# A two-layer network and a conditioned block on one core: the order of the first stage, and the form of the last products

## What is computed

```python
def rmsnorm(x, g):
    y = xf * lax.rsqrt(jnp.mean(xf * xf, axis=-1, keepdims=True) + EPS)
    return (y * g.astype(jnp.float32)).astype(x.dtype)

def pool_mixer(h, w, scale):          # windows 2, 4, 8, 16; a quarter of the columns each
    cs = jnp.cumsum(xg, axis=1)
    outs.append((cs - lag) / cnt - xg)
    ...
    return mixed * scale

def hyena_filters(...):
    hid = jnp.sin(fr * (z @ w1.astype(f32) + b1.astype(f32)))
    hid = jnp.sin(fr * (hid @ w2.astype(f32) + b2.astype(f32)))
...
for i in range(DEPTH):
    a = rmsnorm(h, norm_mix[i])
    h = h + mix
    h = h + swiglu(rmsnorm(h, norm_ffn[i]), ffn_w_gate[i], ffn_w_up[i], ffn_w_down[i])
...
return rmsnorm_2(x, final_g)
```

## Time and profile before

| | us |
|---|---|
| median of 3 runs | 1026.26 (1025.77 to 1027.43) |
| the profiled execution | 1026.83 |
| its span | 1025.0 |
| TensorE busy (matmuls) | 985.7, 96% of the span |
| VectorE busy | 825.7, 81% |
| ScalarE busy | 564.7, 55% |
| GpSimd busy | 110.3, 11% |

### The profile page before, as it was taken

The page is one execution under the profiler, slowest core; times in us unless marked ns, Lnnn a source line. Parts: engine busy times, 40 slices in busy tenths (PEclk is TensorE's granted clock), DMA queues, the critical chain, the costliest instruction groups (busy, mean ns, idle before and its releaser), DMA issues.

```text
span 1025.0 us, 19503 instructions
## 1 busy us (share of the span) xinstructions
PE 985.7 (96%) x7946; PEld 953.8 (93%) x7946; DVE 825.7 (81%) x1388; ACT 564.7 (55%) x1062; POOL 110.3 (11%) x130
## 2 busy tenths in 40 slices
PE   6999999999999999999999999999999999999996
PEld 5999999999888889999999998888999999999995
DVE  7988898887898876999979878888998668776543
ACT  5755454345767656555555535665554466665432
POOL 3100000111000004002203210222001100000001
PEclk9999999999999999999999999999999999999998
DMA  7555557665433334798868814333336436655441
GB/s 239 223 193 212 195 216 255 241 247 206 145 107 120 104 103 166 294 325 302 290 216 298 302 64 160 132 113 111 127 145 209 161 123 221 211 187 182 153 160 42
DMA packets 33881, 192.19 MB, mean 187 GB/s; under 512 B 4976, under 2 KB 6272, under 8 KB 15104
## 3 DMA queue, kind: packets, MB, share of 16 engines
q1 hardware_dynamic: 23440, 157.36, 42.9%
q10 hardware_dynamic: 6912, 25.17, 7.3%
q0 software_dynamic: 3440, 8.42, 2.6%
HBM read 187.78 MB, written 3.15 MB: 186 GB/s over the span
## 4 chain that ended last, share of the span: by engine, by line
PE 70%; DVE 19%; ACT 6%; issue 3%; DMA 2%; POOL 0%; DVEq 0%; ACTq 0%; POOLq 0%
PE ps L93 69%; DVE wl L70 6%; ACT wh L67 2%; DVE a L70 1%; PE ps L96 1%; DMA raw<-w 1%; DVE b L70 1%; ACT s L67 1%; DVE natl L70 1%; DVE s L84 1%; DMA fz<-fz 1%; DVE s L77 1%; DVE xt L73 1%; DVE x L73 0%; DVE x L70 0%
## 5 line engine op out<-in xcount | busy, mean ns | idle before, releaser
L70 DVE TENSOR_TENSOR wl<-raw,wh 128x1024 fp32r<-128x1024 f32 x283 | 341.9, 1223 | 24.4 <-ACT wh L67 23.9
L67 ACT ACTIVATE wh<-raw 128x1024 fp32r<-128x1024 f32 x286 | 296.2, 1049 | 28.3 <-DMA raw<-w 11.1
L93 PE MATMUL ps<-xh,wh 128*128 128x256 f32 (+1 forms) x992 | 278.6, 281 | 3.6 <-DVE wl L70 2.5
L93 PE MATMUL ps<-xh,wl 128*128 128x256 f32 (+1 forms) x992 | 277.1, 279 | 0.0
L93 PE MATMUL ps<-xl,wh 128*128 128x256 f32 x992 | 275.9, 278 | 0.0
L93 PE MATMUL ps<-xt,wh 128*128 128x272 f32 (+1 forms) x1120 | 218.3, 290 | 4.7 <-DVE ps L70 1.5
L93 PEld LDWEIGHTS ps<-xh,wh 128*128 128x128 f32 x992 | 186.9, 188 | 4.8 <-issue 2.4
L93 PEld LDWEIGHTS ps<-xl,wh 128*128 128x128 f32 x992 | 187.3, 189 | 0.0
L93 PEld LDWEIGHTS ps<-xh,wl 128*128 128x128 f32 x992 | 186.9, 188 | 0.2
L93 PEld LDWEIGHTS ps<-xt,wh 128*128 128x128 f32 x1120 | 177.3, 188 | 8.0 <-issue 3.7
L93 PE MATMUL ps<-xt,wl 128*128 128x272 f32 (+1 forms) x560 | 159.9, 286 | 0.0
(11 more groups left out here) (351 smaller groups left out, 1603.6 us busy)
## 6 DMA issues: line engine op xcount, KB each, us to landing
raw<-w SPq DMA_DIRECT2D x141, 1024.0 KB, 5.0
ada<-ada ACTq DMA_DIRECT2D x42, 512.0 KB, 4.5
cb<-ada ACTq DMA_DIRECT2D x6, 512.0 KB, 4.6
raw<-w SPq DMA_DIRECT2D x4, 512.0 KB, 6.3
spare<-w SPq DMA_DIRECT2D x2, 1024.0 KB, 8.6
spectra<-ev POOLq DMA_DIRECT2D x8, 256.0 KB, 3.6
skew<-rpb POOLq DMA_DIRECT2D x8, 192.0 KB, 3.6
x<-x POOLq DMA_DIRECT2D x2, 544.0 KB, 9.5
```

What stands on the lines that cost most here:

```text
L67: return Issued(self.e and self.e.activation(out, src, func, **kw))
L70: return Issued(self.e and self.e.tensor_tensor(out, a, b, op))
L93: return Issued(self.e and self.e.matmul(out, stat, mov, start=start, stop=stop))
```

## The change

- `WARM`, the number of squares of ones, is 13 instead of 20.
- In `start_dve` the sum of squares of token tile 1 comes first, then the four scalings `gw` (with their wait for `cst`), then steps 0 to 2 of the filter network, then the inverse root.
- Steps 3 to 6 of the filter network stand in `first_dve` at f = 0, behind the four `up_out`.
- The output is four VectorE products over two tiles each (128x2x256, `r` repeated for both); GpSimd has none, `final` and its semaphore are gone.

```diff
-WARM = 20
+WARM = 13
...
         V.memset(self.ones[:, :], 1.0 / 1024).then_inc(S["st_v"], ("ones",))
-        for k in range(4):
-            self.mlp_dve(V, 0, k)
         V.wait_ge(S["ld_xt1"], ("load",))
         V.wait_ge(S["st_v"], ("pre",))
         V.ttr(self.sqt[1][:, :], self.xtok[1][:, :], self.xtok[1][:, :], 1.0, 0.0, ALU.mult, ALU.add,
               sm[0:96, 65:66]).then_inc(S["st_v"], ("ssq",))
-        for k in range(4, 7):
+        V.wait_ge(S["ld_cst"], ("load",))
+        for g in range(4):
+            V.ts(sm[:, 88 + 2 * g:90 + 2 * g], self.col("norm_mix0", 2 * g, 2), 1.0 / (2 << g), None,
+                 ALU.mult).then_inc(S["st_v"], ("gw", g))
+        for k in range(3):
             self.mlp_dve(V, 0, k)
...
-        V.wait_ge(S["ld_cst"], ("load",))
-        for g in range(4):
-            V.ts(sm[:, 88 + 2 * g:90 + 2 * g], self.col("norm_mix0", 2 * g, 2), 1.0 / (2 << g), None,
-                 ALU.mult).then_inc(S["st_v"], ("gw", g))
...
             if f == 0:
                 for k in first:
                     self.up_out(V, 0, "f0", self.R[1], T1, *k)
+                for k in range(3, 7):
+                    self.mlp_dve(V, 0, k)
...
         self.rsqrt_dve(V, "out", self.R[0], self.ps[7][:, :TR], TR)
-        for d in range(DT):
-            if d not in (2, 6):
-                self.final(V, d, "out_v")
-
-    def final(self, E, d, done):
-        S, x = self.S, self.x_tile(d, M0, TR)
-        E.wait_ge(S["norm_v"], ("r", "out"))
-        E.wait_ge(S["out_a"], ("x", d))
-        E.tt(x, x, self.R[0][:, :TR], ALU.mult).then_inc(S[done], ("y", d))
+        x = self.X[:, :].rearrange("p (d t) -> p d t", d=DT)
+        for d in range(0, DT, 2):
+            y = x[:, d:d + 2, M0:]
+            V.wait_ge(S["norm_v"], ("r", "out"))
+            V.wait_ge(S["out_a"], ("x", d + 1))
+            V.tt(y, y, self.R[0][:, :TR].unsqueeze(1).broadcast_to([128, 2, TR]), ALU.mult).then_inc(
+                S["out_v"], ("y", d))
...
             self.norm_acc(G, "out", d, TR)
-        for d in (2, 6):
-            self.final(G, d, "out_g")
...
-            for i in (d, d + 1):
-                D.wait_ge(S["out_g" if i in (2, 6) else "out_v"], ("y", i))
+            D.wait_ge(S["out_v"], ("y", d))
```

More of the change, by code:

```diff
@@ L143 @@
            "ada_a ada_v sb_p sb_a sb_v sb_g ctx_a ctx_v ctx_g na_p na_a na_v na_g hy_p hy_a hy_v hy_g "
-           "mod_v out_a out_v out_g").split()
+           "mod_v out_a out_v").split()
 class Stream:
```

## The result

| | before | change |
|---|---|---|
| median (lowest to highest), 4 runs each | 1026.82 (1025.77 to 1027.43) | 1021.90 (1019.99 to 1023.10) |
| the profiled execution | 1026.83 | 1023.10 |
| its span | 1025.0 | 1020.8 |

A forecast was written before the change was run, and what follows sets the result against it. TensorE was taken as nearly always busy, with VectorE and ScalarE setting its pace at a few points. Terms -4.8 + 0 + 1.7 - 0.8 = -3.9 us, from the median 1026.26 to 1022.3; range 1020.8 to 1024.6.

The forecast's parts named there:

- Part 1: Start on VectorE: token-tile square ahead of the filter network, roots at 9.67 instead of 11.92; -2.25 us.
- Part 2: Moved `norm_mix0` scalings: first correction not stopped by GpSimd's rest, 20.40 becomes 15.6; -4.8 us in all, 2.55 from the stall.
- The rival that GpSimd's rest would stop the corrections: First stage: the correction at 15.6 stalls as the scalings did, saving only -1.35 us, time 1024.9; chance 0.07.
- Part 3: TensorE's start: 13 squares for 20 end at 12.4 instead of 13.9, about when the first `al` is ready; cost 0.
- the clock rival: First stage: 13 squares leave TensorE at its lower clock level; all 96 products affected give +7 us, 1033; chance 0.04.
- Part 4: First up group: the network's last four steps ahead of `fh` delay it, with GpSimd stalls of 0.55 us each; +1.7 us.
- Part 5: Kernel's end: four wide output products for six on VectorE and two on GpSimd, last store leaves earlier; -0.8 us.
- The lead was to be 3.1 at 140 us: Sign to look for: TensorE runs some 3.1 us ahead of the kernel before at 140 us.
- The waits for `fu` were expected to stay: Sign in the up groups: TensorE's `fu` waits, 1.3 us between 46 and 140 us before, keep the same size.
- given back further on: Rival, after the first stage: growing delays or a TensorE pause lose 1.5 to 3 us, time 1023.8 to 1025.3; chance 0.16.

The follow-up runs named there:

- seven steps ahead: The change with all seven filter-network steps ahead of the inverse roots, none left in the first feed-forward; one run, 1021.47 us, span 1019.3.
- the last version: The change with network steps 0 to 3 around the roots, 4 and 5 ahead of the feed-forward's inverse norm, 6 behind `fh`; 1018.88 us, ratio 0.9932.
- the third execution of the change: The changed kernel, unedited, measured again in the batch of the final network-step placement; 5 runs, 1021.40 us, ratio 0.9949.

## Why the prediction was right

The forecast was 1022.3 within 1020.8 to 1024.6; it became 1021.9. But the sum is right partly by luck: two things that it did not have, of about 2 us each, cancel.

- **Part 1** (-2.25): the square at 6.03, the scalings at 8.31 and the roots at 9.69, forecast 9.67. The start moves between executions, though: `cst` let the scalings begin anywhere from 8.21 to 8.87 in the executions that have them there, which moves the roots by as much.
- **Part 2** (-4.8 in all): the correction at 15.56 (forecast 15.6) and -4.88 at TensorE. Shown by the scalings alone (2.6, forecast 2.55), and its reason by the step that was put next to a correction. The rival that GpSimd's rest would stop the corrections falls with it.
- **Part 3** (cost 0): the term that the runs contradict. "The squares end at 12.4", because the level rises at 11.2 in the middle of them: the first pooling product stands at 13.28. The squares kept 0.21 us apart until 12.9 in this execution, and the change of level came anywhere from 11.1 to between 13.5 and 14.1 in the executions with 13 or 20 squares. One trace's moment was taken for a property of the kernel. What saved the first stage is that the products behind the squares have some slack. So the chance of 0.04 for the clock rival was too low for its reasons: the margin is no "more than five of the 13". Two executions (seven steps ahead, and the last version) left their squares still at the lower level and lost nothing by it; with 3 squares the rival costs about 3.5 us. The seven squares more cost 0.6 at the end of the stage, not 1.5 and not nothing, and 1.7 at 133 us. So the cut of the squares, put at nothing by itself, goes with the largest gain that the forecast did not have (see "what was missing").
- **Part 4** (+1.7): 4.88 - 3.44 = 1.44. The step had two cases, 1.45 with one stall by GpSimd and 2.0 with two, and 1.7 was the mean of them; one happened, at the clip. Both of GpSimd's rests stretched a VectorE instruction (0.85 and 1.72 us), but the second found a weight rest that ScalarE's work covers. The mistake was to take a mean of two cases that exclude each other.
- **Part 5** (-0.8): -0.75 to the landing of the last store, both in the change and by putting the old form back; -0.91 and -0.92 to the end of the issues. The product of 512 columns takes 686 ns, forecast 0.68.
- **What was missing.** The lead was to be 3.1 at 140 us; it was 5.4. The waits for `fu` were expected to stay: that of 0.98 at 85.35 went, +1.2 us, and that for `ev` fell by 0.77. SyncE issues three loads one behind the other from 73.19 before, and from 69.77 in the change; ScalarE's next cast waits for the first of them (ScalarE's timeline, before and change):

```profile
79.25 1.06 ACT L67 ACTIVATE wh<-raw 128x1024 fp32r<-128x1024 f32 x1 [4.73 <-DMA raw<-w]
```

```profile
74.61 1.06 ACT L67 ACTIVATE wh<-raw 128x1024 fp32r<-128x1024 f32 x1 [3.51 <-DMA raw<-w]
```

  The cast starts 6.06 us after the first issue before and 4.84 in the change; 6.1 with only the scalings moved, 5.6 with twenty squares, 4.7 to 4.8 in the eight others. The lead over before grows by just that. The three executions with the late landing are those with 20 squares, the nine others have 13 or 3. The traces also hold a likely reason, which no run tested: every 13 to 19 us the DMA queue that the profile calls instruction moves one packet of 16 KB, which takes about 1 us. With 20 squares it starts 3.2 us (before), 2.7 (scalings alone) and 1.1 (twenty squares) after the first load's issue, well before that load has landed; in the nine others it starts 4.5 us after the issue or later, when the load is all but there. If this packet holds the load up, the 1.2 us belong to the cut from 20 to 13 squares. That is argued, not shown.
- **Given back**: 1.9 us between 530 and 582, by the wider spacing. It is of the size of "given back further on", but by none of the mechanisms named there (a late bank, a late cast, a pause at 645); the slow stretch was worth nothing where it fell.

So -4.88 + 1.44 - 0.75 = -4.19 is what the edits do at their places, against a forecast -3.9; the regains add about 2.0 and the spacing takes about 1.9.

## What to carry to other kernels

Before moving an instruction beside GpSimd's work, look at where its operands lie. On this chip, VectorE's forms with a PSUM operand ran beside a GpSimd product unchanged, and those with two SBUF tensors, or the scalar form from SBUF to SBUF, waited it out, so that a tiny instruction showed a duration of 2.4 us; once GpSimd's product was the longer one instead (2.62 us for 0.93). Follow a change of few us by the start times of one and the same product in both traces, since a single execution's time can be 2 us off by something else. And a step that is "off the path" where it stood is not free where it goes: the move of four steps won 1.66 us at one place and paid 1.44 at another, and only places where VectorE waited anyway and GpSimd did not work beside it gave both. Last, a term put at nothing deserves a run of its own: the squares stood for 1.7 us.

## What the hardware showed that was not expected

- **Two spacings at one granted clock.** The same 256-column products stand 0.113 or 0.118 us apart at a granted clock of 1.00: 267 or 268 against 257 or 258 in the 30 us from 545. Of the twelve traces, two had the narrow spacing there (before, twenty squares); the third with 20 squares (scalings alone) and all nine with 13 or 3 had the wide one, so a link with the number of squares is not excluded. From 960 to 1000 us it is chosen anew: x355 or x356 in five traces (twenty squares, seven steps ahead, three squares, the last version and the third execution of the change), x342 in seven, the other two executions of the change among them. So there at least it is no property of the kernel. It is worth some 14 products of 0.118, 1.7 us, in 40 us. What chooses it is open.
- **The level of TensorE's clock** was reached between 11.1 and about 14 us by eleven executions that had begun their squares between 7.7 and 8.5, and the granted clock in the windows read 1.00 throughout, at the lower rate too. There, only the spacing of unbroken work shows the level (squares 0.21 or 0.11 us apart; 7 or 10 products in one us with three squares). In a stretch with waits the count shows nothing: before has 5 records from 14 to 15 us, at the higher level.
